# Expert weights in one ring of ten places, filled in order of use

## What is computed

```python
# t: [256, 1024]; w_gate, w_up: [32, 1024, 512]; w_down: [32, 512, 1024]
g = argmax(t @ w_grp + b_grp)                       # one of 4 groups
top_w, top_idx = top 2 of the 8 experts of group g  # weights: softmax x group probability
combine = sum(one_hot(expert_ids, 32) * top_w)      # [256, 32]
for e in range(32):
    hid = silu(t @ w_gate[e]) * (t @ w_up[e])
    out += combine[:, e:e+1] * (hid @ w_down[e])
```

## Time and profile before

| | |
|---|---|
| median of three runs | 2070.7 us |
| profiled execution, its own time | 2072.16 us |
| its span | 2070.0 us |
| TensorE matmul busy | 1915.6 us (93% of the span), x11326 |
| TensorE weight loads busy | 993.0 us (48%) |
| VectorE, ScalarE busy | 553.7 us (27%), 366.3 us (18%) |
| transferred | 727.28 MB, 351 GB/s over the span |
| mean granted TensorE clock | 0.992 |

### The profile page before, as it was taken

One profiled execution on the slowest core, in us unless ns is written; L12 is line 12 of the kernel. 1 busy time (PEld: TensorE's weight loads), 2 busy tenths in 40 slices (PEclk: granted clock), 3 DMA queues, 4 the chain that ended last, 5 costly groups with the idle time before them and its releaser, 6 DMA issues. The chain is left out here.

```text
span 2070.0 us, 28526 instructions
## 1 busy us (share of the span) xinstructions
PE 1915.6 (93%) x11326; PEld 993.0 (48%) x11326; DVE 553.7 (27%) x1285; ACT 366.3 (18%) x822; POOL 3.1 (0%) x7
## 2 busy tenths in 40 slices
PE   6998999998888899999988888999999999989887
PEld 3444555444444345555544444455555555544443
DVE  1334422211122224422212112324544211111112
ACT  2332200000001232300000000224322211111111
POOL 0000000000000000000000000000000000000000
PEclk9999999999999999999999999999999999999999
DMA  9989799999999965799999999742237899999996
GB/s 360 290 279 372 314 422 425 424 427 424 427 424 389 323 240 214 309 423 425 424 426 425 426 425 424 218 149 82 82 122 316 369 425 424 426 425 426 425 426 277
DMA packets 128785, 727.28 MB, mean 351 GB/s; under 512 B 19279, under 2 KB 25658, under 8 KB 79562
## 3 DMA queue, kind: packets, MB, share of 16 engines
q1 hardware_dynamic: 127416, 725.48, 86.9%
q10 hardware_dynamic: 1298, 0.78, 0.2%
HBM read 724.39 MB, written 1.84 MB: 351 GB/s over the span
## 5 line engine op out<-in xcount | busy, mean ns | idle before, releaser
L296 PE MATMUL psum<-arena,norm_w 128*64 128x256 f32 x6144 | 700.3, 381 | 52.3 <-DMA arena<-in_moe_w_dram 31.8
L296 PEld LDWEIGHTS psum<-arena,norm_w 128*64 128x64 f32 x6144 | 434.0, 137 | 317.3 <-issue 54.9
L327 PE MATMUL psum<-arena,hT 128*64 128x512 f32 x1536 | 351.3, 599 | 35.6 <-DMA arena<-in_moe_w_dram 21.8
L408 DVE TENSOR_TENSOR hT<-psum,arena 64x512 f32<-64x512 f32 x128 | 88.1, 689 | 521.4 <-PE psum L327 520.5
L327 PEld LDWEIGHTS psum<-arena,hT 128*64 128x64 f32 x1536 | 107.8, 137 | 245.7 <-issue 222.8
L491 ACT ACTIVATE hT<-psum 128x256 f32<-128x256 f32 x96 | 36.8, 383 | 1004.9 <-PE psum L296 1004.9
L347 PE MATMUL psum<-hT 128*128 128x512 f32 x384 | 177.6, 605 | 7.7 <-DVE hT L408 6.0
L2373 PE MATMUL psum<-arena,hT 128*128 128x512 f32 (+1 forms) x352 | 153.0, 584 | 0.5 <-DVE hT L2724 0.5
L347 PEld LDWEIGHTS psum<-hT 128*128 128x128 f32 x384 | 69.0, 189 | 97.9 <-issue 85.0
L749 DVE COPY hT<-psum 128x256 f32<-128x256 f32 x96 | 40.8, 425 | 261.7 <-PE psum L315 261.7
L2373 PEld LDWEIGHTS psum<-arena,hT 128*128 128x128 f32 x352 | 65.1, 192 | 67.9 <-issue 65.2
(11 more groups left out here) (428 smaller groups left out, 1224.2 us busy)
## 6 DMA issues: line engine op xcount, KB each, us to landing
arena<-in_moe_w_dram SPq DMA_DIRECT2D x192, 2048.0 KB, 36.3
arena<-in_w_gate_dram SPq DMA_DIRECT2D x32, 2048.0 KB, 33.7
arena<-in_w_up_dram SPq DMA_DIRECT2D x32, 2048.0 KB, 35.1
arena<-in_w_down_dram SPq DMA_DIRECT2D x32, 2048.0 KB, 31.1
arena<-in_ada_w_dram SPq DMA_DIRECT2D x24, 2048.0 KB, 15.1
arena<-in_w_in_dram SPq DMA_DIRECT2D x10, 2048.0 KB, 8.1
arena<-in_odd_w_in_dram SPq DMA_DIRECT2D x6, 2048.0 KB, 10.3
arena<-in_even_w_in_dram SPq DMA_DIRECT2D x4, 2048.0 KB, 20.8
```

The costliest lines, as they stand in the source:

```text
L296: m = nc.tensor.matmul(out[64 * half:64 * half + 64, :], xw[:, u, c, :], w[:, c, half * HALF:(half + 1) * HALF], start=(c == 0), stop=(c = ...
L327: m = nc.tensor.matmul(bank_Y[64 * half:64 * half + 64, :], hTs[:, k % 2, (k // 2) * 64:(k // 2) * 64 + 64], experts.slots[slot][2][:, k, ...
L408: return nc.vector.tensor_tensor(y[BLOCK * u:BLOCK * (u + 1), half, :], bank_Y[rows, :], gate2[rows, half * 512:half * 512 + 512], ALU.mult)
```

## The change

- The nine places and a tenth become one ring. A block's number is its turn in use: 0, 1 for w1(0), w3(0); then 3e-1 for w1(e), 3e for w3(e), 3e+4 for w2(e). Block j lies in place j mod 10. The tenth place is the memory of x and h, now one tensor `xh`.
- At the stage's start, SyncE issues w1(2), w3(2), and at `x_kept` w1(3) where w2(2) stood; then a new one, w3(3) into `xh`, once all 16 gathers are done (`gathered`). On the first `w1_used` it issues w2(2), and so on by block number.
- In the loop every refill waits for the use of the block ten numbers before. The body holds ten experts and runs twice; ten are written out ahead of it and two behind it, on SyncE and on TensorE.
- At the end SyncE issues by block number too: w1(30), w3(30), w2(29), w1(31), w3(31), w2(30), w2(31). The order in which TensorE uses them there isn't changed.
- The following mixer's first blocks are all issued on the last `w1_used`.

```diff
-    SLOTS = 3
-    LOADS = tuple(len(range(slot, E, 3)) for slot in range(3))
+    PLACES, AHEAD = 10, ((0, 0), (1, 0), (0, 1), (1, 1), (2, 0), (0, 2), (1, 2), (2, 1), (0, 3), (1, 3))
+    @staticmethod
+    def block(kind, e):
+        return kind if e == 0 and kind < 2 else 3 * e + (-1, 0, 4)[kind]
...
-        self.slots = [(mem["w1b"][:, u], mem["w3b"][:, u], mem["w2b"][:, u]) for u in range(2)] + [extra]
+        up, down = (lambda ap: ap.rearrange("p c n -> p (c n)")), (lambda ap: ap.rearrange("p k n -> p (k n)"))
+        self.places = [up(mem["w1b"][:, 0]), up(mem["w3b"][:, 0]), up(mem["w1b"][:, 1]), up(mem["w3b"][:, 1]), down(mem["w2b"][:, 0]),
+                       up(extra[0]), up(extra[1]), down(mem["w2b"][:, 1]), down(extra[2]), mem["xh"]]
+        blocks = [self.block(kind, e) for kind in range(3) for e in range(E)]
+        self.loads = [sum(j % self.PLACES == at for j in blocks) for at in range(self.PLACES)]
...
+    def load_w1(self, sp, e, k=0):
+        at = self.block(0, e) % self.PLACES
+        sp.dma_start(self.up_tile(at), self.w1[e % 2, k * 5 + e // 2]).then_inc(self.landed[at], 16)
...
@@ sync @@
-        experts.load_up(sp, 2, 0, 1)
+        experts.load_w1(sp, 2)
+        experts.load_w3(sp, 2)
         sp.wait_ge(x_kept, 4)
-        experts.load_down(sp, 2, 0, 1)
+        experts.load_w1(sp, 3)
+        sp.wait_ge(gathered, len(GATHERS))
+        experts.load_w3(sp, 3)
         sp.wait_ge(steps_ready, 1)
         rounds = steps(sp)
         with sp.Fori(0, rounds) as r:
-            def refill_down(k, off):
-                sp.wait_ge(down_done, r * E + k * 6 + (off - 2))
-                experts.load_down(sp, off % 3, off % 2, k * 3 + off // 2)
-            def refill_up(k, off):
-                slot, u, pair, done = off % 3, off % 2, k * 3 + off // 2, r * E + k * 6 + (off - 2)
-                sp.wait_ge(w1_used, done)
-                experts.load_w1(sp, slot, u, pair)
-                sp.wait_ge(up_done, done)
-                experts.load_w3(sp, slot, u, pair)
-            def refill(k, off):
-                refill_up(k, off)
-                if not (isinstance(k, int) and k * 6 + off == 3):
-                    refill_down(k, off - 1)
-            for off in range(3, 6):
-                refill(0, off)
-            with sp.Fori(1, E // 6) as k:
-                for off in range(6):
-                    refill(k, off)
-            last = E // 6
-            refill(last, 0)
-            refill_down(last, 0)
-            refill_up(last, 1)
-            refill_down(last, 1)
+            def refill(k, e):
+                done = r * E + k * 10
+                if e > 4:
+                    sp.wait_ge(down_done, done + (e - 4))
+                else:
+                    sp.wait_ge(up_done, done + 1)
+                experts.load_w1(sp, e, k)
+                sp.wait_ge(w1_used, done + (e - 2))
+                experts.load_w3(sp, e, k)
+                sp.wait_ge(up_done, done + (e - 2))
+                experts.load_down(sp, e - 1, k)
+            sp.wait_ge(w1_used, r * E + 1)
+            experts.load_down(sp, 2)
+            for e in range(4, 10):
+                refill(0, e)
+            with sp.Fori(0, 2) as k:
+                for e in range(10, 20):
+                    refill(k, e)
+            refill(0, E - 2)
+            refill(0, E - 1)
+            sp.wait_ge(up_done, r * E + (E - 2))
+            experts.load_down(sp, E - 1)
             with sp.If(rounds > r + 1):
 
                 sp.wait_ge(down_done, r * E + E)
-                for slot, u, pair in ((0, 0, 0), (1, 1, 0), (2, 0, 1)):
-                    experts.load_up(sp, slot, u, pair)
-                    experts.load_down(sp, slot, u, pair)
+                for kind, e in experts.AHEAD:
+                    (experts.load_w1, experts.load_w3, experts.load_down)[kind](sp, e)
         if following is not None:
-            for n, freed in zip(range(following.AHEAD), (w1_used, up_done, down_done)):
-                sp.wait_ge(freed, rounds * E)
+            sp.wait_ge(w1_used, rounds * E)
+            for n in range(following.AHEAD):
                 following.load(sp, n)
...
@@ tensor @@
-            def turn_of(k, off):
-                return off % 3, r * experts.LOADS[off % 3] + k * 2 + (off // 3 + 1)
+            def place_of(kind, k, e):
+                j = experts.block(kind, e)
+                return j % experts.PLACES, r * experts.loads[j % experts.PLACES] + k * 3 + (j // experts.PLACES + 1)
 
             def step(k, off):
 
-                e = base + (k * 6 + off)
-                slot, nth = turn_of(k, off)
-                before = turn_of(k, off - 1) if off else turn_of(k - 1, 5)
-                u, second = off % 2, isinstance(k, int) and k * 6 + off == 1
-                up_first(e, u, slot, nth, second)
-                q = r * PAIRS + (k * 3 + off // 2)
+                e = base + (k * 10 + off)
+                u, second = off % 2, off == 1
+                up_first(e, u, *place_of(0, k, off), second)
+                q = r * PAIRS + (k * 5 + off // 2)
                 if u == 0:
                     turn_sel(q - 1)
                 elif not second:
                     pe.wait_ge(selT_copied, q)
                 turn(e - 1)
-                up_second(u, slot, nth)
+                up_second(u, *place_of(1, k, off))
                 if u == 1 and not second:
                     scatter(q - 1)
-                down(e - 1, *before, second)
-            up_first(base, 0, *turn_of(0, 0), True)
-            up_second(0, *turn_of(0, 0))
-            for off in range(1, 6):
+                down(e - 1, *place_of(2, k, off - 1), second)
+            up_first(base, 0, *place_of(0, 0, 0), True)
+            up_second(0, *place_of(1, 0, 0))
+            for off in range(1, 10):
                 step(0, off)
-            with pe.Fori(1, E // 6) as k:
-                for off in range(6):
+            with pe.Fori(0, 2) as k:
+                for off in range(10, 20):
                     step(k, off)
-            last, q = E // 6, r * PAIRS + (PAIRS - 1)
-            step(last, 0)
+            q = r * PAIRS + (PAIRS - 1)
+            step(0, E - 2)
             pe.wait_ge(selT_copied, q)
             scatter(q - 1)
             turn(base + (E - 2))
-            down(base + (E - 2), *turn_of(last, 0))
-            up_first(base + (E - 1), 1, *turn_of(last, 1))
-            up_second(1, *turn_of(last, 1))
+            down(base + (E - 2), *place_of(2, 0, E - 2))
+            up_first(base + (E - 1), 1, *place_of(0, 0, E - 1))
+            up_second(1, *place_of(1, 0, E - 1))
             turn_sel(q)
             turn(base + (E - 1))
-            down(base + (E - 1), *turn_of(last, 1))
+            down(base + (E - 1), *place_of(2, 0, E - 1))
...
@@ program @@
-    x, h, hT = (nc.alloc_sbuf_tensor(n, s, F32)[:, :, :] for n, s in (("x", [P, TILES, D]), ("h", [P, TILES, D]), ("hT", [P, DC, TOK])))
+    xh, hT = nc.alloc_sbuf_tensor("xh", [P, 2 * TILES * D], F32)[:, :], nc.alloc_sbuf_tensor("hT", [P, DC, TOK], F32)[:, :, :]
+    x, h = (xh[:, i * TILES * D:(i + 1) * TILES * D].rearrange("p (t d) -> p t d", t=TILES) for i in range(2))
```

More of the change, by code:

```diff
@@ L94, in __init__, with up_tile, down_tile, load_w3 @@
         self.w2 = w2.rearrange("(j two) (half p c) n -> two j p half c n", two=2, half=2, p=P)
[L96 to L108, removed]
+    def up_tile(self, at):
+        return self.places[at].rearrange("p (c n) -> p c n", c=DC)
+    def down_tile(self, at):
+        return self.places[at].rearrange("p (k n) -> p k n", k=FF // P)
+    def load_w1(self, sp, e, k=0):
+        at = self.block(0, e) % self.PLACES
+        sp.dma_start(self.up_tile(at), self.w1[e % 2, k * 5 + e // 2]).then_inc(self.landed[at], 16)
+    def load_w3(self, sp, e, k=0):
+        at = self.block(1, e) % self.PLACES
+        sp.dma_start(self.up_tile(at), self.w3[e % 2, k * 5 + e // 2]).then_inc(self.landed[at], 16)
+    def load_down(self, sp, e, k=0):
+        at = self.block(2, e) % self.PLACES
+        sp.dma_start(self.places[at].rearrange("p (half c n) -> p half c n", half=2, c=2),
+                     self.w2[e % 2, k * 5 + e // 2]).then_inc(self.landed[at], 16)
     def load_router(self, sp):
@@ L117, in prefetch @@
         self.load_router(sp)
-        for u in range(2):
-            self.load_up(sp, u, u, 0)
-            self.load_down(sp, u, u, 0)
+        for e in range(2):
+            self.load_w1(sp, e)
+            self.load_w3(sp, e)
+            self.load_down(sp, e)
 def expert_stage(nc, stage, experts, x, h, hT, gate1, scale2, shift2, gate2, norm_w, consts, mem, ps, x_banks, turn_banks, following=None, store=None,
@@ L289, in tensor, with up @@
             nc.tensor.matmul(XG[n % len(XG)][:, 0:PICKS], h[:, t, c * P:(c + 1) * P], sel[t], start=True, stop=True).then_inc(gathered, 1)
-        def up(w, out, landed, used, u, slot, nth):
-            pe.wait_ge(landed[slot], nth * 16)
+        def up(out, used, u, at, nth):
```

(17 more changed lines are left out.)

25 lines of the change are left out of this document (12 added, 13 removed).

## The result

The changed kernel takes 2083.24 us (median of 5 runs, 2082.02 to 2088.97) against 2070.7 for the kernel before on the same chip (5 runs): a ratio of 1.0071, interval 1.0053 to 1.009. It is slower, by 12.5 us. The profiled execution has a span of 2081.5 us, 11.5 more than before.

What follows compares the result with a forecast made beforehand. The stream of expert weights at 425 GB/s was taken to bound each stage, plus TensorE's work behind its last wait. -14.7 (early block) + 17.7 (wait) + 3.6 (clock) = +6.6 us on 2070.7, so 2077, range 2069 to 2086.

Steps and rivals of the forecast that it cites:

- w2(30) behind w3(31): At each stage's end, w2(30) comes as third block after w2(29), so TensorE waits 5.2, 5.2 and 7.3 us: +17.7 us.
- no wait for w2(30): Rival, chance 0.12: at the stage's end w2(30) is there when TensorE reaches it, only the early start's gain is left: 2056.
- The clock: Behind the wait for w2(30), TensorE's clock falls to half: 1.2 us a stage, bounds 0 and 1.7, +3.6 us in all.
- w3(3) on the gather's end: At each stage's start, issuing this block sooner restarts the stream of transfers earlier: 4.9 us a stage, -14.7 us in all.
- Refills by block number: In the long stretch, transfers already queue up at a rate of 425 GB/s, so issuing in this order changes nothing.
- The same holds for the body of ten experts: fewer jumps back on an engine with slack: In the stage's loop, the longer body costs or gains nothing, since no jump costs a pause now.
- the front: The stage's start, where the early w3(3) lets the stream of transfers begin sooner: -14.7 us in all.
- If that cover were gone (a faster stream), jumps would count: Caveat on the loop: jumps back cost nothing only while TensorE has slack against the transfers; no size given.
- Tenth place brings nothing: Rival, chance 0.04: at the stage's start w3(3) starts the stream no sooner, the end's cost stands alone: +21 us, 2092.
- The two ends cancel: Rival, chance 0.24: start gains 15.2 us, clock stays up, end's wait is 17.7 us or somewhat shorter: 2070 to 2073.

Runs made afterwards that it cites:

- e1: The changed kernel with SyncE issuing w2(30) ahead of w1(31) and w3(31), in TensorE's order of use: 2059.32 us, ratio 0.9935.
- e2: The kernel before with one change, SyncE issuing w2(30) behind w3(31): 2091.52 us, ratio 1.0101.
- e7: The changed kernel with TensorE's last step regular (w1(31), w3(31), then w2(30)), SyncE's order left as it is: 2064.25 us, ratio 0.9971.
- e4: The changed kernel without the early block: w3(3) issued on the first `w1_used`, just ahead of w2(2): 2093.53 us, ratio 1.011.
- e3: The kernel before with a loop body of twelve experts run twice, in place of six run four times, on SyncE and TensorE: 2081.96 us, ratio 1.0057.
- e6: The kernel before with TensorE's loop over bodies of six written out, so no jump inside a stage: 2073.99 us, ratio 1.0013.
- e8: The changed kernel with the tenth place used once a stage, nine places behind it, body of six, last blocks issued in order of use: 2061.86 us, ratio 0.9947.

## Why the prediction was right and where it was wrong

The direction and the range held; the total was 6 us short, and that closeness hides a larger miss. That it lies inside the range is luck: the mixers came out 5.9 us shorter, which nothing in the sum had foreseen. Without that the median would have stood near 2089 (2083.2 and 5.9, an estimate), above the range.

- *w2(30) behind w3(31)*: right in mechanism, in place and nearly in size, +16.3 for 17.7. w2(30) started 14.8 us after w2(29) in all three stages, so stage 3's wait was 5.9 and not 7.3: the 16.2 us that I had dated there before wasn't a pace of the stream. (In that trace the lag of the last engine rose from 2.1 to 3.5 us at that very block, w3(31), behind a page that started 2.6 us before it landed.) e1, e2 and e7 show it by itself. w2(30) landed at 429.7 in stage 1 and TensorE began at 429.9; blocks did not overtake each other, so the rival *no wait for w2(30)* is out. By the Trainium skill's rule (DMA: Bandwidth & Descriptors, Queues, rings and completion order) order of completion isn't guaranteed; in no run here did a block whose landing the trace dates land out of turn, though the 16 parts of a block came over 6 us apart.
- *The clock*: mis-sized. I took 1.2 us a stage with 1.7 as the upper bound and 3.6 in all; it was 2.7, 1.8 and 2.5, so 7.1. The bound came from a single row (5.35 us in place of 3.65), and the clock stays at 0.50 for longer than that, 6.8 us in stages 1 and 2 and 10.2 in stage 3: w2(30) takes 6.37 us in place of 3.65, which is 2.7 by itself. The Trainium skill's rule that I weighed (TensorE: Matmul & The Clock Gate, HAM oscillation), a long wait for DMA and then half clock, pointed the right way; the trace agrees, with 0.50 at 654 to 656 behind a wait of 5.73.
- *w3(3) on the gather's end*: right in mechanism. It was issued 0.03 us after the gather's end, transfers ran from there, and the first engine shows the full 5.1 us at w2(29). The sum had -14.7 for it, and e4 gives 13.5 in this kernel. (Its upper bound of 5.05 us a stage, 15.2 in all, was the smallest of the three dates; they add up to 15.4.)
- *Refills by block number, "The same holds for the body of ten experts: fewer jumps back on an engine with slack"*: **this is the step that failed.** I costed the body at nothing by looking at the jumps, and the window cited for them, 250 to 300 us, holds none: the first jump back is at 370. (The conclusion was right, the kernel before doesn't pause there.) What I left out is that a body of ten no longer stays with TensorE from one pass to the next, so that its instructions are fetched again; the pages take turns with the weights on single DMA engines, and the slowest engine sets when each block lands. Of the front's 14.7 us only 6.0 were left at w2(29), 8.7 less. e4 splits that: 7.4 for what the change costs without the early block, which e3 (7.8) and e6 (8.1) show to be the fetched code without any ring, and 1.2 that the early block itself fell short. The short body of e8 got back 4.5 of the 8.7; the 4.2 that its front still falls short are its own lag, which is open above. I had the sentence "If that cover were gone (a faster stream), jumps would count"; the cover on TensorE held (at the jumps back it paused 15.6 us in all, and the wait for transfers that came later took them up), the cover that was missing was on the DMA engines.
- *The mixers*: I had nothing there, and the third came out 5.4 us shorter, within the spread of the ten traces. Without that and the 0.5 us by which stage 1 started sooner, the change would have cost the stages' 17.3. That is luck.
- *Tenth place brings nothing* is out (e4, e8). *The two ends cancel* is out too: the front's gain fell short of it, and wait and clock came to 23.4.

So -14.7 + 17.7 + 3.6 = +6.6 was in truth -6.0 + 16.3 + 7.1 - 5.9 in the mixers = +11.5.

## What to carry to other kernels

When a stream of transfers bounds a stage, give the consuming engine and the issuing engine the same order down to the last block, and check it where a hand-written end departs from the loop. Before a loop body is lengthened, count the instruction pages of a pass in the long stretch: they share the DMA engines with the data, and one late engine delayed every block behind it here for as long as the queue was full. And ask of a block fetched early which blocks behind it come sooner; if none does, nothing is gained.

## What was not expected of the hardware

**TensorE keeps a body of six and not one of ten.** In 300 to 480 us the kernel before fetches 4 instruction pages, all of them ahead of 354 us, in the first pass of its body, and then none for 280 us: the three further passes. (That these pages are TensorE's shows in e6, where only TensorE's loop is written out and the pages go on through the stage.) In that stretch the changed kernel fetches 10:

```profile
q8 instruction: 10, 0.16, 0.4%
```

In the first pass of its body the kernel before starts 4 pages, the changed one 7 and the body of twelve (e3) 9, so some 66, 115 and 147 KB; this is an estimate, as the parts of a page at either end aren't counted. The Trainium skill (Runtime: NRT & Kernel Launch, Instruction fetch mechanics) gives TensorE 128 KiB for instructions, refilled in blocks of 16 KiB. The bodies of six and of twelve agree with that; the body of ten is near that size and decides nothing. The same section says that the store is but two lines of 16 KiB with purely sequential prefetch, and that a branch out of them must fetch. The trace disagrees for TensorE: the body of six takes at least four pages and jumps back three times (at 370.0, 454.5 and 543.2 us) with none fetched and no pause.

**A jump back to code that has to be fetched costs 3 to 5 us.** The jump back of the changed kernel's body pauses TensorE by 3.4, 3.3 and 3.6 us (3.43 at 482.86), in stage 3 once more by 5.3, though a page's own packet takes 1.1. That the full weight queue makes the fetch slow isn't shown: no run has such a jump beside an idle queue. The clock falls to 0.50 behind it in all three stages (in e4's stage 1 a pause of 3.1 us left it at 1.00). It costs nearly nothing while TensorE is ahead of the transfers.

**The parts of a block land up to 6 us apart**, and the gap stays as long as the queue is full, for 400 us in these stages.
